# Order of the three partial products of a pair in a split-weight matmul stream

## What is computed

```python
def swiglu(x, w_gate, w_up, w_down):
    return (jax.nn.silu(x @ w_gate) * (x @ w_up)) @ w_down

# PEER, per block of 128 tokens
act = jax.nn.gelu(jnp.einsum('tkd,td->tk', u_emb[eb], tb), approximate=False) * gb
return jnp.einsum('tk,tkd->td', act, v_emb[eb])
```

## Time and profile before

| | |
|---|---|
| median of three runs | 2194.47 us (2194.3 to 2196.11) |
| the profiled execution's own time | 2196.2 us |
| its span | 2194.4 us |
| PE busy with matmuls | 2147.0 us, 98% of the span, 18,016 matmuls |
| PE weight loads (PEld) | 2034.0 us, 93%, 18,016 loads |
| DVE, ACT, POOL busy | 1601.9, 1038.2, 335.1 us |
| HBM read | 363.85 MB |

### The profile page before, as it was taken

How to read it: one execution, slowest core, us unless ns; L and a number is a source line. 1 busy time by engine, 2 the same in 40 slices (tenths; PEclk the granted TensorE clock), 3 DMA queues, 4 the chain that set the end, 5 groups by cost and what they waited for, 6 DMA issues and landing times. The chain is left out here.

```text
span 2194.4 us, 46339 instructions
## 1 busy us (share of the span) xinstructions
PE 2147.0 (98%) x18016; PEld 2034.0 (93%) x18016; DVE 1601.9 (73%) x3068; ACT 1038.2 (47%) x1687; POOL 335.1 (15%) x199
## 2 busy tenths in 40 slices
PE   9999999999999999999899999999999998999998
PEld 9999989999999998999889989999999997888887
DVE  6665868765875687876686687699799555777776
ACT  5444555443544466554453345454444453333333
POOL 0000000000000000000000000199877871000000
PEclk9999999999999999999999999999999999999999
DMA  6553535564556443556332226577555675666664
GB/s 218 181 197 131 195 111 175 181 200 147 168 179 200 136 167 128 175 193 220 117 124 70 79 81 210 170 243 239 154 146 145 178 187 176 204 206 209 206 204 162
DMA packets 134106, 373.70 MB, mean 170 GB/s; under 512 B 44568, under 2 KB 48808, under 8 KB 133808
## 3 DMA queue, kind: packets, MB, share of 16 engines
q1 hardware_dynamic: 118320, 364.95, 50.5%
q0 software_dynamic: 15616, 6.35, 2.4%
HBM read 363.85 MB, written 7.39 MB: 169 GB/s over the span
## 5 line engine op out<-in xcount | busy, mean ns | idle before, releaser
L1180 DVE TENSOR_TENSOR w_lo<-ring,w_hi 128x1024 fp32r<-128x1024 f32 (+1 forms) x301 | 393.3, 1308 | 186.0 <-ACT w_hi L926 185.4
L926 ACT ACTIVATE w_hi<-ring 128x1024 fp32r<-128x1024 f32 (+1 forms) x301 | 337.5, 1126 | 335.2 <-PE ps L554 321.9
L554 PE MATMUL ps<-x_hi,w_hi 128*128 128x272 f32 (+1 forms) x1608 | 460.4, 286 | 1.4 <-DVE x_lo L1251 1.1
L554 PE MATMUL ps<-x_hi,w_lo 128*128 128x272 f32 (+1 forms) x1608 | 458.1, 285 | 0.0
L554 PE MATMUL ps<-x_lo,w_hi 128*128 128x272 f32 (+1 forms) x1608 | 455.8, 283 | 0.0
L554 PEld LDWEIGHTS ps<-x_hi,w_hi 128*128 128x128 f32 x1608 | 302.2, 188 | 4.5 <-DVE w_lo L1180 1.5
L554 PEld LDWEIGHTS ps<-x_lo,w_hi 128*128 128x128 f32 x1608 | 302.0, 188 | 0.2
L554 PEld LDWEIGHTS ps<-x_hi,w_lo 128*128 128x128 f32 x1608 | 302.2, 188 | 0.0
L3391 ACT ACTIVATE v_gated_hi<-ring 128x1024 fp32r<-128x1024 f32 x128 | 135.9, 1062 | 226.8 <-PE ps L3441 226.3
L3176 POOL MEMSET hot_j<- 128x768 f32 x1 | 0.7, 737 | 1417.2 <-POOLq L3000 1417.2
L3441 PE MATMUL ps<-v_gated_hi,gated_gelu_hi 128*128 128x512 f32 x512 | 203.0, 396 | 7.6 <-DVE v_gated_lo L266 7.6
(11 more groups left out here) (531 smaller groups left out, 5279.8 us busy)
## 6 DMA issues: line engine op xcount, KB each, us to landing
ring<-in_gate_up SPq DMA_DIRECT2D x173, 512.0 KB
ring<-in_peer_v SPq DMA_DIRECT2D x128, 512.0 KB
ring<-in_down SPq DMA_DIRECT2D x64, 704.0 KB
ring<-in_peer_u_mid SPq DMA_DIRECT2D x80, 512.0 KB
ring<-in_peer_u_early SPq DMA_DIRECT2D x48, 512.0 KB
ring<-in_w_in SPq DMA_DIRECT2D x46, 512.0 KB
ring<-in_project SPq DMA_DIRECT2D x32, 512.0 KB
ring<-in_da_qk SPq DMA_DIRECT2D x18, 512.0 KB
```

The costliest lines, as they stand in the source:

```text
L554: mm = nc.tensor.matmul(ps[:, bank, 0:ntok], parts[left][:, item % SLOTS, t * P:(t + 1) * P], rhs[right][:, k, 0:ntok], start=start and n ...
L926: A.activation(parts_of(n)[0][:, n % SLOTS, 0:width[n]], ring[:, n % SLOTS, 0:width[n]], ACT.Copy).then_inc(hi_done.sem, 1)
L1180: V.tensor_tensor(parts_of(n)[1][:, n % SLOTS, 0:width[n]], ring[:, n % SLOTS, 0:width[n]], parts_of(n)[0][:, n % SLOTS, 0:width[n]].bitca ...
```

## The change

A second tuple `LOW_FIRST` names the same three products with lo weights by hi tokens first, then hi weights by hi tokens and hi weights by lo tokens. Three places use it instead of `TERMS`: `pe_linear`, `products` of the first block, and the keys of PEER. In the value stage the tuple stays, but the loops are exchanged: each kind of product is done for both row halves before the next kind. The number of matmuls, their operands and the semaphores are the same. The tuple adds a line, so lines behind L304 move on by one.

```diff
-                    for n, (left, right) in enumerate(((0, 0), (0, 1), (1, 0))):
+                    for n, (left, right) in enumerate(LOW_FIRST):
...
 TERMS = ((0, 0), (0, 1), (1, 0))
+LOW_FIRST = ((1, 0), (0, 0), (0, 1))
...
             def products(item, t, k, bank, ntok, rhs, start, stop):
                 parts = parts_of(item)
-                for n, (left, right) in enumerate(TERMS):
+                for n, (left, right) in enumerate(LOW_FIRST):
...
                 for k in range(KD):
-                    for n, (left, right) in enumerate(TERMS):
+                    for n, (left, right) in enumerate(LOW_FIRST):
...
                     for tb in range(2):
-                        for hf in range(2):
-                            for n, (left, right) in enumerate(TERMS):
+                        for n, (left, right) in enumerate(TERMS):
+                            for hf in range(2):
                                 mm = nc.tensor.matmul(ps[:, 2 * tb + hf, :], gated_gelu[left][:, b, P * tb:P * tb + P],
```

## The result

The change made the kernel slower: 2215.02 us (median of four runs, 2214.64 to 2217.78) against 2194.99 us before (four runs), a ratio of 1.0091 with a 95% interval of 1.0078 to 1.0104, or +20.0 us. The forecast was no change, in a range of 2184 to 2200 us. The profiled execution took 2214.6 us with a span of 2212.8 us, 18.4 us more than the 2194.4 us of before.

The account below looks back on a forecast made before the run. PE was taken as the bound, running matmuls for 98% of the span. Linear terms 0, value stage -0.5 us and waits unchanged took the median 2194.47 to 2194.0 us, forecast as no change within 0.2%, range 2184 to 2200 us.

Parts of the forecast that it names:

- Linear stages, 0: Wide and narrow linear matmuls (10,392): same pairs of streamed and loaded tile, every kind keeps its price, 0 us.
- (a): Linear stages: reading the same tokens twice in a row is cheap, so faster, -8.4 us, 2185.6 us; chance 0.25.
- (b): Wide and value stages: the repeated weight load collides, so slower, +6.0 us, 2200.5 us; chance 0.15.
- (c): Value stage: a repeated weight load is dropped, -6.6 us or more, 2187.9 us; chance 0.03.
- the 2.4 us allowed: Narrow linear steps: allowance of 0.5 ns on each of 4,776 matmuls, either way, as kinds lie near their mean.
- Value stage, -0.5 us: Value stage, 1,536 matmuls: six products take 1,386.9 instead of 1,389.0 ns, 256 times, -0.5 us.
- I price them by the tile that is loaded: Value stage: two new pairs without a row priced by loaded tile, 231.6 ns for gelu_hi, at most 229.2 for gelu_lo.
- the bound named there, +3.4 us: Value stage: upper bound with all 1,536 steps at the dearest kind, 233.7 ns, +3.4 us.
- The value term of rival (b), +1.1 us: Value stage: four of six steps, those loading gelu_hi, cost 233.7 ns, +1.1 us.
- Waits: All four changed places: no wait added or removed; the 7.6 us wait before the value stage stays.
- the slower side: Whole kernel: the outcome slower than no change, given only to the colliding repeated load, 2200.5 us; chance 0.15.
- The range: Whole kernel time: 2184 to 2200 us, taking in the -8.4 us case and leaving out the -15 us end.

## Why the prediction was wrong, by its steps

*Linear stages, 0.* Right for the wide ones, and not quite for the narrow ones. In the changed kernel the wide kinds are 122.7 (behind x_hi by w_hi), 122.6 (behind x_lo) and 125.0 ns (behind x_hi by w_lo); the forecast said that the same pairs keep their prices. Rivals (a) and (b) fell: reading the same tokens twice is neither cheaper nor dearer. So did (c): there are still 18,016 loads. But the narrow price came from a window of L283 alone, where the steps run evenly. In the later key items they do not, and PE's last matmul of the keys started 2.0 us earlier with the change (1817.90 against 1819.93), 1.1 us of it from the items behind 1,713 us. That lies within the 2.4 us allowed, for a reason that the allowance did not have.

*Value stage, -0.5 us.* Wrong in sign and small: +1.8 ns a step, +2.8 us. The step that failed is "I price them by the tile that is loaded". The two new pairs cost 234.7 and 235.0 ns, not 231.6 and 229.2. It lay within the bound named there, +3.4 us. The value term of rival (b), +1.1 us, had the sign right and was still too small.

*Waits.* This step made the prediction wrong: "Nothing is queued differently on SP, ACT, DVE or POOL, so no wait is added or removed. The 7.6 us wait in front of the value stage stays". It grew to 26.2 us. No instruction moved on the other engines, but their times did. The later key items became 1% shorter (2.77 to 2.74 us between subtractions on average), and POOL answered with a step, not in proportion. I had read the wait of 7.6 us as a fixed cost and did not ask who ends it. The page of before answered that in its chain of work, which I left out of my reading:

```profile
PE ps L3441 16%; POOL far_gates L3188 8%; PE ps L283 4%; DMA far_gates<-far_gate,far_index 1%; POOL u_early_lo L266 1%; PE ps L3138 0%; DMA ring<-in_peer_u_mid 0%; DVE gate_map L3422 0%; ACT u_early_hi L260 0%; DMA far_in<-far_gates 0%; POOL far_gates L3181 0%; ACT L3220 0%; DVE v_gated_lo L266 0%; ACT gate_map L3396 0%; ACT u_mid_hi L3202 0%
```

Not PE but POOL's indirect DMAs and their landings stand in the chain from 1566 to 1829 us, with PE busy for all of 1566 to 1820 us beside them. With that row the slower side had a mechanism with a price: POOL has next to no slack there, its DMAs lie between 1.42 and 2.47 us, and each that moves from one to the other costs 1 us.

*The range.* It held the linear and value terms and no cost for another engine, so 2215 lay 15 us outside.

What stays open is why lo weights first shortens the odd key items. Start times show that there the lo part is ready only about when the last matmul of the item before starts, so the first load comes late behind that matmul: instead of 3 ns, 26 or 67 to 87 before the change and 21 to 26 with it. The 67 to 87 ns follow the subtractions that took 1.27 to 1.29 us because a DMA of POOL's had just started, so POOL holds up PE too. The item then takes 2.81 or 2.85 us before the change and 2.77 or 2.75 with it: with the old order the distances stay at 115 to 123 ns for up to twelve matmuls behind the first one, with the new for up to six. Which overlap of stream and load does this was not tried.

## What to carry to other kernels

Before a wait is called fixed, ask in the chain of work who ends it: an engine that is 15% busy over the span can set the end of a stage in which TensorE has no pause. Where two engines hold each other up and both run in a cycle, the cost of a small change of pace is a step; compare the length of the held cycle (here 1.23 + 1.29 + 0.30 = 2.82 us) with the other's period (here 2.72 to 2.85 us), and where they lie as close as these, within 4%, give the range a term for it. In such a place, more work on the engine that isn't the bound, or a shorter instruction on the one that holds, can win back more than it costs: 39 extra matmuls took 15 us off here.

## What the runs showed that I had not expected

An indirect DMA of 96 single elements takes GpSimd 1.42 us, but 2.47 us when issued 0.05 us behind the start of a subtraction of 1,024 columns with two inputs in SBUF. Issued up to 0.03 us behind the start it is still free: a few hundredths of a microsecond decide. And the distance between two matmuls of 512 columns lies between 229.2 and 235.7 ns, by which tile streams, which is loaded meanwhile and what went before (v_hi while gelu_hi is loaded takes 230.5 to 235.7 in one kernel), whereas a change of PSUM bank at each matmul costs nothing with the pairs kept (231.5 ns both ways).
